# Final scaling of a decoder trunk split between VectorE and GpSimd, and an earlier product for the sum of squares

## The reference

```python
h2 = rmsnorm(x, g_ffn[l]) * (1 + sc2) + sh2
gate, up = jnp.split(jnp.dot(h2, w_gu[l]), 2, axis=-1)
x = x + g2 * jnp.dot(jax.nn.silu(gate) * up, w_down[l])
...
y = rmsnorm(x, g_final)

def rmsnorm(x, g):
    xf = x.astype(jnp.float32)
    y = xf * lax.rsqrt(jnp.mean(xf * xf, axis=-1, keepdims=True) + EPS)
    return (y * g.astype(jnp.float32)).astype(x.dtype)
```

## Time and profile before

| what | value |
|---|---|
| median of 3 runs | 2430.22 us (2428.72 to 2431.3) |
| the profiled execution's own time | 2430.17 us |
| its span, first instruction to last | 2428.0 us |
| granted TensorE clock, mean | 0.986 of full speed |
| TensorE matmuls busy | 2319.4 us, 96% |
| VectorE busy | 1551.2 us, 64% |
| ScalarE busy | 922.2 us, 38% |
| GpSimd busy | 238.6 us, 10% |
| final scaling, sixteen operations | 11.22 us, from 2413.84 |

### The profile page before, as it was taken

The page is one execution under the profiler, slowest core; times in us unless marked ns, Lnnn a source line. Parts: engine busy times, 40 slices in busy tenths (PEclk is TensorE's granted clock), DMA queues, the critical chain, the costliest instruction groups (busy, mean ns, idle before and its releaser), DMA issues.

```text
span 2428.0 us, 44374 instructions
## 1 busy us (share of the span) xinstructions
PE 2319.4 (96%) x18645; PEld 2172.0 (89%) x18645; DVE 1551.2 (64%) x2240; ACT 922.2 (38%) x1328; POOL 238.6 (10%) x289
## 2 busy tenths in 40 slices
PE   5679999999999999899999999999999989999996
PEld 1179888888897999899999999999999989999996
DVE  0442642333335223787887888788778778888898
ACT  2122442423234222654444444444444433333443
POOL 3150140000000111100000000000000211011131
PEclk9889999999999999999999999999999999999998
DMA  9956455656563433223443443344344676365552
GB/s 336 332 177 210 155 155 191 217 169 214 176 227 107 172 114 103 109 103 137 169 153 119 159 156 128 137 169 161 118 162 154 259 262 228 133 216 189 181 215 89
DMA packets 191079, 422.43 MB, mean 174 GB/s; under 512 B 14693, under 2 KB 116885, under 8 KB 188833
## 3 DMA queue, kind: packets, MB, share of 16 engines
q1 hardware_dynamic: 171072, 341.35, 40.8%
q0 software_dynamic: 17216, 73.78, 8.7%
q10 hardware_dynamic: 2592, 4.46, 0.5%
HBM read 365.45 MB, written 54.08 MB: 173 GB/s over the span
## 4 chain that ended last, share of the span: by engine, by line
PE 91%; DMA 3%; DVE 2%; issue 2%; ACT 1%; POOL 0%; SPq 0%; DVEq 0%; POOLq 0%; ACTq 0%
PE PJ L2339 28%; PE PS L2339 28%; PE PJ L1960 25%; DMA AR<-in_weights 3%; PE PJ L1913 2%; PE PJ L1903 1%; PE PJ L2304 1%; PE PS L2195 1%; PE PJ L1925 1%; PE PJ L2281 1%; DVE HS L1802 0%; PE PS L2304 0%; DVE X L1880 0%; PE PS L2233 0%; PE PS L2198 0%
## 5 line engine op out<-in xcount | busy, mean ns | idle before, releaser
L2339 PE MATMUL PS<-HS,WO 128*128 128x272 f32 x5376 | 687.0, 289 | 10.5 <-issue 9.8
L2339 PEld LDWEIGHTS PS<-HS,WO 128*128 128x128 f32 x5376 | 682.0, 189 | 12.0 <-issue 12.0
L2339 PE MATMUL PJ<-HS,WO 128*128 128x272 f32 x5376 | 683.6, 289 | 0.0
L2339 PEld LDWEIGHTS PJ<-HS,WO 128*128 128x128 f32 x5376 | 680.4, 189 | 0.0
L1120 ACT ACTIVATE WO<-GR 128x1024 fp32r<-128x1024 f32 (+1 forms) x462 | 477.1, 1033 | 512.0 <-PE PS L2339 247.3
L1655 DVE TENSOR_TENSOR WO<-GR,WO 128x1024 fp32r<-128x1024 f32 (+1 forms) x462 | 555.8, 1203 | 120.3 <-ACT WO L1120 120.2
L1960 PE MATMUL PJ<-HH,WH 128*128 128x272 f32 x1568 | 345.8, 302 | 7.3 <-issue 2.5
L1960 PE MATMUL PJ<-HL,WH 128*128 128x272 f32 x1568 | 325.5, 289 | 0.0
L1960 PE MATMUL PJ<-HH,WL 128*128 128x272 f32 x1568 | 325.5, 289 | 0.0
L1279 DVE TENSOR_TENSOR WL<-RW,WH 128x1024 fp32r<-128x1024 f32 x102 | 132.7, 1305 | 271.1 <-ACT WH L855 270.8
L1960 PEld LDWEIGHTS PJ<-HH,WH 128*128 128x128 f32 x1568 | 247.2, 190 | 41.2 <-issue 33.2
(11 more groups left out here) (311 smaller groups left out, 1867.8 us busy)
## 6 DMA issues: line engine op xcount, KB each, us to landing
GR<-in_weights SPq DMA_DIRECT2D x264, 512.0 KB, 6.7
AR<-in_weights SPq DMA_DIRECT2D x256, 256.0 KB, 4.5
RW<-in_weights SPq DMA_DIRECT2D x102, 512.0 KB, 4.5
HS<-act_parts POOLq DMA_DIRECT2D x91, 544.0 KB, 6.2
act_parts<-SQ SPq DMA_DIRECT2D x40, 952.0 KB, 6.9
AR<-in_weights SPq DMA_DIRECT2D x64, 512.0 KB, 5.4
MIX<-in_xT SPq DMA_DIRECT2D x1, 4352.0 KB, 17.6
X<-in_xT POOLq DMA_DIRECT2D x4, 1088.0 KB, 10.4
```

Of the source, the lines that this page charges most:

```text
L2339: mm = e.matmul(out, w[part], HS[:, HS_AT[QUARTER[i]], y, (2 * first + k) % (KT // 2), :], start=OPENS[i] and k == 0 and x == 0, stop=k == ...
```

## The change

The last five tiles (POOL_LAST = 5, tiles 11 to 15) are scaled by GpSimd instead of VectorE, in two operations each. The first, tensor_scalar by the column of g_final, is issued behind GpSimd's last addition, each waiting for the square of its tile; it counts on the semaphore cs_zero. The second, tensor_tensor by RNF, waits for both reciprocals (rstd) and counts on the new semaphore fin_pool. VectorE scales tiles 0 to 10. SP stores the tiles in the same order as before and waits for fin or fin_pool. On TensorE the two products of ACF with ones are issued first, once the additions into ACF are done, and the two of QXF after the wait for the last square.

```diff
@@ -136,6 +136,7 @@
 X1_STEPS = KT + 2
 X1_SUMS = KT - 1
 EARLY = 8
+POOL_LAST = 5
 SQUARES_AT = 1
 SUM_AT = 3
 H_AT = 5
@@ -506,7 +507,7 @@
 
         "t_made af_hi af_lo parts_out "
 
-        "table fin y_out").split()
+        "table fin fin_pool y_out").split()
     S = {n: ctx.enter_context(nc.semaphore(n)) for n in names}
     raw = [ctx.enter_context(nc.semaphore(f"raw{i}")) for i in range(RAW)]
     ada_in = [ctx.enter_context(nc.semaphore(f"ada_in{i}")) for i in range(AS)]
@@ -644,7 +645,10 @@
             if s + 2 < STEPS:
                 load_group(s + 2)
         for k in range(KT):
-            sp.wait_ge(S["fin"], k + 1)
+            if k < KT - POOL_LAST:
+                sp.wait_ge(S["fin"], k + 1)
+            else:
+                sp.wait_ge(S["fin_pool"], k - (KT - POOL_LAST) + 1)
             sp.dma_start(outs["yT"][:, k, :], X1[:, k, :]).then_inc(S["y_out"], 16)
         sp.wait_ge(S["y_out"], 16 * KT)
 
@@ -842,6 +846,15 @@
                 for v in range(11, 14):
                     if last_use(v - 4) == STEPS - DOWN + u:
                         load_parts(STEPS - DOWN + u, i, v)
+        at = PRM["g_final"][0]
+        for k in range(KT - POOL_LAST, KT):
+            g.wait_ge(S["x1_sq"], X1_STEPS + k + 1)
+            g.tensor_scalar(X1[:, k, :], X1[:, k, :], PR[:, at + k:at + k + 1], None, ALU.mult)\
+                .then_inc(S["cs_zero"], 1)
+        g.wait_ge(S["rstd"], 6)
+        for n, k in enumerate(range(KT - POOL_LAST, KT)):
+            g.wait_ge(S["cs_zero"], 2 + n)
+            g.tensor_tensor(X1[:, k, :], X1[:, k, :], RNF[:, :], ALU.mult).then_inc(S["fin_pool"], 1)
 
 
 
@@ -1876,7 +1889,7 @@
             d.reciprocal(RNF[:, HT * w:HT * w + HT], RNF[:, HT * w:HT * w + HT]).then_inc(S["rstd"], 1)
         d.wait_ge(S["rstd"], 6)
         g = PRM["g_final"][0]
-        for k in range(KT):
+        for k in range(KT - POOL_LAST):
             d.scalar_tensor_tensor(out=X1[:, k, :], in0=X1[:, k, :], scalar=PR[:, g + k:g + k + 1], in1=RNF[:, :],
                                    op0=ALU.mult, op1=ALU.mult).then_inc(S["fin"], 1)
 
@@ -2344,8 +2357,13 @@
             for i in range(7):
                 product(s, i)
         e.wait_ge(S["x1_acc"], X1_SUMS + KT)
-        e.wait_ge(S["x1_sq"], X1_STEPS + KT)
-        sum_squares(PS, ACF, QXF)
+        for n, x in enumerate((ACF, QXF)):
+            if n:
+                e.wait_ge(S["x1_sq"], X1_STEPS + KT)
+            for w in range(2):
+                mm = e.matmul(PS[:, w, 0:HT], ones, x[:, HT * w:HT * w + HT], start=(n == 0), stop=(n == 1))
+                if n:
+                    mm.then_inc(S["sum_done"], 1)
 
 
 # ---- launch: the inputs laid out for the program, one core, the outputs put back ------------------
```

## The result

The changed kernel takes 2436.88 us in the median of 15 runs (2429.65 to 2440.58), the kernel before 2430.22 in 15 runs beside it. The ratio is 1.0025, with a 95% interval of 1.0017 to 1.0033, so some 4 to 8 us more; the forecast was 2435.8 us. The profiled execution took 2435.28 us, its span 2433.5, against 2430.17 and 2428.0.

The account below looks back on a forecast made before the run. TensorE bounds the kernel, with VectorE and DMA engines bounding its end; -0.54 + 0.5 + 2.4 + 3.6 - 0.35 (less backlog) = +5.6 us on 2430.22 gave 2435.8 us, range 2432.5 to 2439.0.

Parts of the forecast that it names:

- Order of the sums: Before T0 (VectorE's first scaling): ACF's products issued before the wait let the first root wait only for QXF's first half, -0.54 us.
- Early products: GpSimd's five products by g_final: each holds VectorE about 0.6 us at its start, making the last square and T0 0.5 late.
- Rival 2: Before T0: each early product holds VectorE for its whole 1.6 us, +4.8 instead of +0.5, 2440.1 us; chance 0.13, partial included.
- Turns in the final scaling: After T0: GpSimd's five multiplies by RNF alternate with VectorE's eleven scalings, each adding 1.17 us to VectorE's row, +2.4 us.
- Rival 1: Final scaling: VectorE is served first, GpSimd only when it is done, 2432.8 us; chance 0.16, including four served in turn.
- Five stores behind tile 10: Final stores: tiles 11 to 15 wait behind tile 10, then leave at the DMA rate, five x 0.73 = 3.6 us.
- One sign: Profile after: stores 11 to 15 issued back to back after tile 10, landings growing by 0.4 us each.
- rival 3: Final scaling: no contention, DMA rate still rules, only the 0.54 gain is left, 2429.7 us; chance 0.11, softer contention included.
- The sum: Whole change: -0.54 + 0.5 + 2.4 + 3.6 - 0.35 (less backlog) = +5.6 us.

Follow-up runs that it names:

- e1: The kernel before with only the new order of the sum of squares, VectorE scaling all sixteen tiles: ratio 1.0002.
- e2: The changed kernel with the old order of the sum of squares, so the split of the scaling alone: ratio 1.0022.
- e7: The kernel before with one unused VectorE reciprocal ahead of the last additions into tile 15, to lengthen TensorE's pause: 2434.63 us in one execution.
- e4: The changed kernel without GpSimd's five early products by g_final: 2431.38 us in one execution.
- e3: The changed kernel with SP storing GpSimd's tiles interleaved with VectorE's instead of after tile 10: ratio 1.0004.
- e5: The changed kernel with ScalarE copying RNF into PSUM and VectorE's eleven scalings reading the norm there: ratio 1.0000.
- e8: The kernel before with the new order of sums and ScalarE's reciprocal square root replacing its root and VectorE's two reciprocals: 2426.47 us, ratio 0.9976.

## Why the prediction was right, step by step

- **Order of the sums, -0.54.** Measured -0.52 (e1). What I did not see is that the clock can fall in TensorE's pause and cost the sums another microsecond (e2, e7). In the profile of the changed kernel the pause before QXF's products is 1.47 us and the clock stays full. The step was right; whether it is worth more beside the split is open: the tails of e2 and the changed kernel differ by 1.5 us, but each is one execution, the fall came at different distances from the last product, and the ratios of whole executions (1.0022 and 1.0025) show no such difference.
- **Early products, +0.5.** Measured 0.48 (after against e4), and 1.64 us each where 1.6 was forecast. They hold VectorE only at their start: the one issued at 2405.57 runs to 2407.4, and X at 2406.41 takes its plain 0.47 inside it. Rival 2 falls with that. The Trainium skill's rule in "SBUF — State Buffer", section "Who interferes with whom", that whoever issues first keeps the shared ports for the whole instruction (a sentence on VectorE's two-port modes there), does not hold for this one-input form. The forecast's 0.6 us ran to the end of the held operation; less its own duration, the hold is about 0.5 us (X at 2407.45 ends at 2408.39, and 0.47 of that is its own work; the second product had begun at 2407.39). The operation held was X at 2407.45, not the SC ahead of it, which slipped in first.
- **Turns in the final scaling.** All five were served in turn. One turn added (13.11 - 10 x 0.696 - 0.77)/5 = 1.08 us instead of 1.17, so VectorE ended at T0 + 13.1 and not 13.6. This is the one term that was mis-sized, by nearly 0.5 us in all. I took its price from a single case beside a VectorE operation of 1,024 columns; that GpSimd's turn is cheaper beside this form is my guess at the reason, not tested. Rival 1 (VectorE first) did not occur in any of the split kernels.
- **Five stores behind tile 10, +3.6.** Measured 3.5: from landing to landing 0.7 us each, and e3 gives back 3.5 by order alone. Tile 10 landed 2.3 us after its issue instead of 2.15. One sign did not come: the landings of the last five were to grow by 0.4 us each, but grew only from 2.3 to 3.2 in all, since SP did not issue them 0.33 us apart but 0.4 to 0.8 (its longest issue took 716 ns). The time from landing to landing, which sets the end, was as forecast.
- **No gain even without contention (rival 3).** e5 is that case: T0 to end 14.20.
- **The sum.** +5.6 forecast for the tail, 5.2 measured; the runs give 4 to 8.

What stays open: when TensorE's clock falls; why GpSimd was served first in e4 and VectorE in the others, though VectorE issued first by some 0.05 us each time; and the part of the median's 6.7 us beyond the tail's 5.2, which lies within the interval.

## What to carry to other kernels

Before an elementwise row is split between two engines, look at what consumes it: here the DMA engines took a tile each 0.73 us and VectorE made one each 0.70, so with stores of one tile no faster scaling could end earlier, while anything finished early but stored late costs the full rate at the end. VectorE operations with two SBUF operands and two-input GpSimd operations take turns rather than overlap (1.08 us a turn here); an operand in PSUM lifts that (e5). Shorten what lies ahead of the first store (e8). Issue what is ready in a pause of TensorE: it gained 0.52 us here (e1), and it leaves fewer products to run slowly should the clock fall.

## What the runs showed of the hardware

- The sums after a pause of 2.0 us ran at TensorE's full granted clock (kernel before), those after 2.4 and 2.48 us (e7, e2) at 0.50, which brought T0 0.9 to 1.0 us later. The clock fell 1.9 us (e2) and 2.5 us (e7) after the last product, so the length of the pause alone does not decide.
- A one-input GpSimd multiply of 544 columns takes 1.64 us, longer than the two-input one (1.34), but holds VectorE's two-SBUF-input operations for some 0.5 us only.
- VectorE's scalings and GpSimd's two-input multiplies, all with both operands in SBUF, took strict turns, 1.08 us for each of GpSimd's; with the norm in PSUM they ran side by side at 0.77 and 1.34 us (e5).
- Stores of 2,176 bytes per partition filled the DMA engines at 382 GB/s; those of 4,352 bytes ran at 402.
